# Three PSUM banks in turn, in place of two, for the gate and up products of three feed-forward layers

## The chip, the core and the metric

The kernel runs on one core of a Trainium2 chip. The metric is the device time of one execution in microseconds (us), the median of several. The core's engines run side by side and wait for one another by semaphores: TensorE (PE in the profile, its weight loads are PEld), VectorE (DVE), ScalarE (ACT), GpSimd (POOL), and SyncE (SP), which here only issues DMAs. Matmul results go to PSUM, a memory of eight banks of 512 fp32 columns in each of 128 partitions.

## The reference, cut to what matters

Two small networks follow one another over x of 256 tokens by 1024 features. The first has a mixer, a cross attention to a memory and a feed-forward layer. The second has two layers, each of an attention, a cross attention to a memory and a feed-forward layer with a short convolution. The three feed-forward layers are these (2816 hidden features, 22 blocks of 128):

```python
def _swiglu(hn, w_gate, w_up, w_down):                       # first network, here "ffn0"
    return (jax.nn.silu(hn @ w_gate) * (hn @ w_up)) @ w_down

def conv_ffn(h, w_up, conv_w, conv_b, w_down):               # second network, "ffn1", "ffn2"
    S = h.shape[1]
    u = h @ w_up
    up = jnp.pad(u, ((0, 0), (CONV_WIDTH_2 - 1, 0), (0, 0)))
    c = conv_b
    for i in range(CONV_WIDTH_2):
        c = c + up[:, i:i + S] * conv_w[i]
    gate, val = c[..., :D_FF_2], c[..., D_FF_2:]
    return (jax.nn.silu(gate) * val) @ w_down
```

## The kernel before

Activations lie feature-major, so a linear layer's output is made in blocks `m` of 128 features by 256 tokens, each of them one accumulator. Every fp32 product is made of three matmuls of rounded parts: weights and inputs are split into a high part and a rest (`w_hi`, `w_lo`; `a_hi`, `a_lo`; `b_hi`, `b_lo`), and `three` (L446) issues high by high, high by rest and rest by high. All weights pass in one fixed order through slots of eight 128 by 128 blocks: SP loads a slot to `w_raw`, ACT makes its high part (L1153), DVE (L1708) or POOL (L2522) its rest, and PE spends 24 matmuls on it. The split slots are a ring of three. Every engine's program is written out by hand in this order, and each engine works strictly in its own order; the helper `ahead(s)` on ACT and DVE makes the parts of slots up to three ahead before the work that belongs to slot `s`.

Each accumulator has a key, such as `("x_o", 7)` or `("ffn0", 3)`, and a bank (`ACC_BANK`). `accumulators` hands out banks in the order of the slots: a key in `fixed` gets that bank, every other takes the next of a cycle over banks 0 and 1. `ACC_BEFORE` is the key that had the same bank last. PE, before the first matmul of a key, waits until the engine that reads that earlier accumulator has done so:

```python
def acc_take(key):
    if ACC_BEFORE[key]:
        pe.wait_ge(*at(("acc", ACC_BEFORE[key])))
    return acc(key)
```

Where a residual is added (`x_o`, the output projection of the first cross attention, has keys 0 to 7), DVE adds accumulator `m` to `h` (L2135), which frees the bank; before it, in DVE's order, stands the rest of a later weight slot (`ahead`, L1708), and after it come `a_lo` of block `m-1` (L1720) and the running sum of squares (L2125). Block `m` of the next layer's input is ready with `a_lo` of `m`. `ffn0` follows `x_o` directly on PE. In a feed-forward layer PE's order for `f` from 0 to 22 is: gate product `f` (key 2f), up product `f` (key 2f+1), down product of `f-1`; the down products add up in banks 4 to 7. Each of these is one slot:

```python
for g in range(2):
    out = acc_take((name, 2 * f + g))[:, 0:T]
    slot_ready(s)
    for k in range(KD):
        if f == 0 and g == 0:
            pe.wait_ge(*at(("a_lo", tag, k)))
        ins = three(out, blocks(s, k), pair(A, k), k == 0, k == KD - 1)
```

After key 0, PE makes the last sum of squares in bank 2 (L533), of which ACT makes the scale `rstd` (L1184, L1186) between two loads of activation tables (L1158, L1161). DVE reads each gate and up accumulator at L2267, times `rstd`, and that read frees its bank. In `ffn1` and `ffn2` the convolution follows on ACT (L1591) and DVE (L2272, L2274); then come SiLU on ACT (L1596), the product on DVE (L2286), and its high part (L1606) and rest (L2295), which the down product reads.

Of the kernel before, what the change touches and what calls it, by code (L numbers as in the profile page):

```python
# [80 lines left out]
KIND = {name: kind for name, kind, _, _ in LINEARS}  # L81
# [2484 lines left out]

def accumulators():

    turn = itertools.cycle((0, 1))
    fixed = {("ab_v", 0, 0): 0, ("ab_v", 0, 1): 1, ("ab_q", 0): 6, ("ab_k", 0): 7, ("ab_q", 1): 6, ("ab_k", 1): 7,  # L2570
             ("ab_o", 0): 7, ("glu", 1): 3, ("glu", 2): 2, ("fox_v", 0, 0): 0, ("fox_v", 0, 1): 1, ("fox_f", 0): 6, ("fox_q", 0): 7,
             ("fox_k", 0): 6, ("fox_q", 1): 7, ("fox_k", 1): 6, ("fox_o", 0): 7}
    seen = set()
    for name, j in SLOT:
        k, m = SHAPE[name]
        if KIND[name] == "tok":
            per = k * min(m, 4) // 8
            keys = [(name, j // per, tt) for tt in range(TT)]
        elif KIND[name] == "ffn":
            keys = [(name, i) for i in range(2 * NF)]  # L2580
        else:
            keys = [(name, i) for i in range(8 * j // k, -(-8 * (j + 1) // k))]
        for key in keys:
            if key not in seen:
                seen.add(key)
                yield key, fixed[key] if key in fixed else next(turn)


ACC_BANK = dict(accumulators())
ACC_BEFORE, _last = {}, {}  # L2590
for _key, _b in ACC_BANK.items():
# [143 lines left out]
```

## Time and profile before

| | |
|---|---|
| median of 3 runs | 1244.7 us (1241.61 to 1245.04) |
| profiled execution, its own time | 1243.67 us |
| its span, first to last instruction | 1241.4 us |
| PE busy | 1188.7 us, 96% |
| PE's weight loads busy | 1117.8 us, 90% |
| DVE, ACT, POOL busy | 809.1, 656.9, 264.8 us |
| PE in the chain that ended last | 82% of the span |
| mean granted TensorE clock | 0.988 of 2.4 GHz |

A busy share is an average over the whole program: what the change is worth is read where the feed-forward layers and their neighbours stand in the trace. The three layers' gate, up and down products lie at about 316 to 507, 678 to 870 and 1035 to 1227 us of the span.

### The profile page before, as it was taken

Reading aid. Unit: us, or ns where it says so; the run is one execution under the profiler, and the core shown is the slowest. Engines: PE = TensorE matmul, PEld = TensorE weight load, DVE = VectorE, ACT = ScalarE, POOL = GpSimd, SP = SyncE. Lnnn points to the kernel's source line nnn. Section 1 sums busy time; section 2 is a strip of 40 time slices with the busy share of each in tenths; the row PEclk is TensorE's granted clock in tenths of the full one; section 3 lists DMA queues with packets and bytes.
Section 4 is the critical chain, followed back from the end, with each engine's and each line's share of the span. In section 5 each row is a group of like instructions: output and inputs, shape, how many; then the busy total and the mean of one; then the engine's idle time right before and its main releaser. Section 6 shows DMA issues by size and latency. Waiting matters only on the chain.

```text
span 1241.4 us, 24075 instructions
## 1 busy us (share of the span) xinstructions
PE 1188.7 (96%) x9808; PEld 1117.8 (90%) x9808; DVE 809.1 (65%) x1427; ACT 656.9 (53%) x1128; POOL 264.8 (21%) x171
## 2 busy tenths in 40 slices
PE   7999998999999999999989999999999988999997
PEld 5888788899999999898887999999889877999997
DVE  4897855754644554667775777776664566776776
ACT  3346455554644444555555555555655566555554
POOL 4030000211223223221130223223212111223231
PEclk9999999899999999999989999999999999999999
DMA  8333333434665555533343465655443332655551
GB/s 331 121 120 104 118 122 136 125 131 135 192 189 182 189 178 179 157 126 108 119 136 102 153 187 174 192 179 187 143 136 117 126 125 87 197 176 186 187 174 48
DMA packets 51660, 188.59 MB, mean 152 GB/s; under 512 B 5728, under 2 KB 5856, under 8 KB 51040
## 3 DMA queue, kind: packets, MB, share of 16 engines
q1 hardware_dynamic: 51552, 187.07, 47.1%
q8 instruction: 78, 1.28, 0.4%
q14 instruction: 30, 0.25, 0.1%
HBM read 186.00 MB, written 1.05 MB: 151 GB/s over the span
## 4 chain that ended last, share of the span: by engine, by line
PE 82%; DVE 8%; ACT 4%; issue 3%; POOL 2%; DMA 0%; DVEq 0%; ACTq 0%; POOLq 0%
PE banks L446 64%; PE banks L476 6%; ACT w_hi L1153 2%; DVE w_lo L1708 2%; PE banks L519 1%; PE banks L948 1%; PE banks L504 1%; POOL w_lo L2522 1%; DVE a_lo L1720 1%; DVE h L2135 1%; DVE gates L2125 1%; PE banks L962 1%; PE banks L567 1%; PE banks L928 1%; PE banks L865 1%
## 5 line engine op out<-in xcount | busy, mean ns | idle before, releaser
L446 PE MATMUL banks<-a_hi,w_hi 128*128 128x256 f32 x1432 | 412.0, 288 | 8.7 <-DVE a_lo L1720 6.3
L2522 POOL TENSOR_TENSOR w_lo<-w_raw,w_hi 128x1024 fp32r<-128x1024 f32 x98 | 238.9, 2439 | 837.7 <-ACT w_hi L1153 837.7
L1153 ACT ACTIVATE w_hi<-w_raw 128x1024 fp32r<-128x1024 f32 x313 | 328.6, 1050 | 155.1 <-PE banks L446 155.0
L446 PE MATMUL banks<-a_lo,w_hi 128*128 128x256 f32 x1432 | 406.0, 284 | 0.0
L446 PE MATMUL banks<-a_hi,w_lo 128*128 128x256 f32 x1432 | 405.8, 283 | 0.0
L1708 DVE TENSOR_TENSOR w_lo<-w_raw,w_hi 128x1024 fp32r<-128x1024 f32 x215 | 267.6, 1245 | 78.6 <-ACT w_hi L1153 78.2
L446 PEld LDWEIGHTS banks<-a_hi,w_hi 128*128 128x128 f32 x1432 | 275.5, 192 | 12.1 <-DVE a_lo L1720 7.2
L446 PEld LDWEIGHTS banks<-a_lo,w_hi 128*128 128x128 f32 x1432 | 275.6, 192 | 0.5
L446 PE MATMUL banks<-b_hi,w_hi 128*128 128x256 f32 x880 | 255.9, 291 | 21.1 <-DVE b_lo L1725 6.6
L446 PEld LDWEIGHTS banks<-a_hi,w_lo 128*128 128x128 f32 x1432 | 275.5, 192 | 0.0
L446 PE MATMUL banks<-b_lo,w_hi 128*128 128x256 f32 x880 | 250.8, 285 | 0.0
L446 PE MATMUL banks<-b_hi,w_lo 128*128 128x256 f32 x880 | 250.7, 285 | 0.0
L446 PEld LDWEIGHTS banks<-b_hi,w_hi 128*128 128x128 f32 x880 | 170.6, 194 | 26.7 <-issue 9.5
L446 PEld LDWEIGHTS banks<-b_lo,w_hi 128*128 128x128 f32 x880 | 170.7, 194 | 0.3
L446 PEld LDWEIGHTS banks<-b_hi,w_lo 128*128 128x128 f32 x880 | 170.6, 194 | 0.0
L1591 ACT ACTIVATE arena<-arena,pars 128x256 f32<-128x256 f32 x88 | 53.0, 602 | 132.1 <-DVE arena L2267 132.1
L2267 DVE TENSOR_TENSOR arena<-banks,rstd 128x256 f32<-128x256 f32 x132 | 55.9, 424 | 102.4 <-PE banks L446 92.5
L2272 DVE SCALAR_TENSOR_TENSOR arena<-arena,pars 128x255 f32<-128x255 f32 x88 | 59.7, 678 | 60.7 <-ACT arena L1591 60.7
L476 PE MATMUL banks<-early,w_raw 128*128 128x256 f32 x368 | 83.8, 386 | 7.7 <-DMA w_raw<-in_weights 7.5
L476 PEld LDWEIGHTS banks<-early,w_raw 128*128 128x128 f32 x368 | 70.2, 193 | 18.4 <-DMA w_raw<-in_weights 7.5
L1179 ACT ACTIVATE a_hi<-h,pars 128x256 fp32r<-128x256 f32 x64 | 32.5, 507 | 64.0 <-DVE h L2135 53.9
L1606 ACT ACTIVATE b_hi<-arena 128x256 fp32r<-128x256 f32 x66 | 27.6, 418 | 37.3 <-DVE arena L2286 37.3
(388 smaller groups left out, 1330.2 us busy)
## 6 DMA issues: line engine op xcount, KB each, us to landing
w_raw<-in_weights SPq DMA_DIRECT2D x342, 512.0 KB, 3.6
arena<-in_mem SPq DMA_DIRECT2D x2, 1024.0 KB, 8.9
h<-in_x SPq DMA_DIRECT2D x1, 1024.0 KB, 5.0
early<-in_mem SPq DMA_DIRECT2D x1, 1024.0 KB, 14.2
out_h<-h SPq DMA_DIRECT2D x4, 256.0 KB, 2.6
cons<-in_cons SPq DMA_DIRECT2D x1, 546.0 KB, 7.5
arena<-in_late SPq DMA_DIRECT2D x1, 448.0 KB, 4.2
pars<-in_pars SPq DMA_DIRECT2D x1, 290.5 KB, 2.9
```

The source lines that it names most:

```text
L446: ins = mm(out, l, r, start=start and n == 0, stop=stop and n == 2, skip_group_check=check)
L476: ins = mm(out, raw(s, b % 8), x[:, k, :], start=n == 0, stop=n == K - 1)
L504: ins = mm(out, x[:, k, cols], raw(s, b * w % 8, w), start=k == 0, stop=k == K - 1)
L519: ins = mm(bank[2][:, 0:T] if out is None else out, ONES_D[:] if by is None else by, squares, start=m == 0, stop=m == KD - 1)
L1153: do(WHI[:, ring(n), :], RAW[:, n % RAW_SLOTS, :], ACT.Copy).then_inc(*inc("w_hi_made", ("w_hi", n)))
L1179: do(x[0][:, m, :], src, ACT.Copy, scale=par(g, m)).then_inc(*inc("input_hi", ("a_hi", tag, m)))
L1591: do(FC[:, 2 * (f % 2) + g, :], FS[:, 2 * (f % 3) + g, :], ACT.Identity, scale=par(f"cw{conv}", 88 + g * NF + f), bias=par(f"cb{conv}", g ...
L1606: do(BH[:, f % 3, :], FA[:, f % 2, :], ACT.Copy).then_inc(*inc("ffn_act_hi", ("act_hi", tag, f)))
L1708: v.tensor_tensor(WLO[:, ring(n), :], RAW[:, n % RAW_SLOTS, :], WHI[:, ring(n), :].bitcast(F32), ALU.subtract).then_inc(*inc("w_lo_made", ...
L2267: v.tensor_tensor(x, acc(t)[:, 0:T], R[:], ALU.mult).then_inc(*inc("ffn_scaled", ("fs", tag, f, g), ("acc", t)))
L2272: step(v.scalar_tensor_tensor(c[:, 1:T], x[:, 0:T - 1], par(f"cw{conv}", 44 + g * NF + f), c[:, 1:T], ALU.mult, ALU.add), label="ffn_conv")
L2522: g.tensor_tensor(WLO[:, ring(n), :], RAW[:, n % RAW_SLOTS, :], WHI[:, ring(n), :].bitcast(F32), ALU.subtract).then_inc(*inc("w_lo_pool", ...
```

## The change

The keys of layers of the kind `"ffn"` take their bank from a cycle of their own, over banks 0, 1 and 3. All other keys go on with the cycle over 0 and 1. An instruction's place in its engine's order is the same on every engine; the bank that some matmuls and reads address differs, and so does the read for which PE waits.

```diff
 def accumulators():
 
-    turn = itertools.cycle((0, 1))
+    turn, of_three = itertools.cycle((0, 1)), itertools.cycle((0, 1, 3))
...
         for key in keys:
             if key not in seen:
                 seen.add(key)
-                yield key, fixed[key] if key in fixed else next(turn)
+                yield key, fixed[key] if key in fixed else next(of_three if KIND[name] == "ffn" else turn)
```

What the tables `ACC_BANK` and `ACC_BEFORE` hold for the first keys of the three layers and for what follows a layer, worked out from the code:

```
key            before: bank, freed by     now: bank, freed by
ffn0, 0        1   x_o, 6                 0   x_o, 7
ffn0, 1        0   x_o, 7                 1   x_o, 6
ffn0, 2        1   ffn0, 0                3   glu, 1
ffn0, 3        0   ffn0, 1                0   ffn0, 0
ffn0, 4        1   ffn0, 2                1   ffn0, 1
ffn0, 5        0   ffn0, 3                3   ffn0, 2
ffn1, 0        0   m_o0, 6                3   ffn0, 41
ffn1, 1        1   m_o0, 7                0   m_o0, 6
ffn1, 2        0   ffn1, 0                1   m_o0, 7
ffn2, 0        1   m_o1, 6                1   m_o1, 6
ffn2, 1        0   m_o1, 7                3   ffn1, 42
ffn2, 2        1   ffn2, 0                0   m_o1, 7
ab_v, 0, 0     0   ffn0, 43               0   ffn0, 42
ab_v, 0, 1     1   ffn0, 42               1   ffn0, 43
```

From key 3 on, a key of these layers waits for the read of the key three before it, where it waited for the one two before it.

## Rows read from the trace of the kernel before

**Rows 1.** The page: span, and busy time of each engine

```profile
span 1241.4 us, 24075 instructions
...
PE 1188.7 (96%) x9808; PEld 1117.8 (90%) x9808; DVE 809.1 (65%) x1427; ACT 656.9 (53%) x1128; POOL 264.8 (21%) x171
```

**Rows 2.** Stretches inside the layers: busy us by engine, granted clock, DMA share, GB/s

```profile
320.00:505.00 185.00, 184.79 (x1533) 184.19 (x1534) 92.29 (x139) 87.64 (x117) 53.01 (x23) 1.00 0.60 186
695.00:870.00 175.00, 175.00 (x1454) 175.00 (x1454) 126.74 (x203) 97.52 (x143) 50.22 (x21) 1.00 0.58 183
1055.00:1226.00 171.00, 171.00 (x1427) 171.00 (x1426) 123.75 (x199) 94.69 (x139) 48.07 (x20) 1.00 0.55 170
```

**Rows 3.** Who waited for L2267 (DVE's read of an accumulator): us, times

```profile
PEld banks L446: 0.2, 1
```

**Rows 4.** Timeline of PE, start of `ffn0`: start us, us, instruction, [idle before, releaser]

```profile
316.31 0.28 PE L446 MATMUL banks<-a_hi,w_hi 128*128 128x256 f32 x1
...
319.94 0.38 PE L446 MATMUL banks<-a_hi,w_hi 128*128 128x256 f32 x1 [1.32 <-DVE a_lo L1720]
320.17 0.28 PE L446 MATMUL banks<-a_lo,w_hi 128*128 128x256 f32 x1
...
321.02 0.27 PE L446 MATMUL banks<-a_hi,w_lo 128*128 128x256 f32 x1
321.13 0.59 PE L533 MATMUL banks<-gates,ones_d 128*128 128x256 f32 x2
```

**Rows 5.** Timeline of DVE, the same stretch and the first products

```profile
317.81 1.23 DVE L1708 TENSOR_TENSOR w_lo<-w_raw,w_hi 128x1024 fp32r<-128x1024 f32 x1 [0.98 <-ACT w_hi L1153]
318.96 0.41 DVE L2135 TENSOR_TENSOR h<-h,banks 128x256 f32<-128x256 f32 x1
319.41 0.48 DVE L1720 SCALAR_TENSOR_TENSOR a_lo<-h,pars,a_hi 128x256 fp32r<-128x256 f32 x1
...
326.96 0.42 DVE L2267 TENSOR_TENSOR arena<-banks,rstd 128x256 f32<-128x256 f32 x1
...
329.33 1.22 DVE L1708 TENSOR_TENSOR w_lo<-w_raw,w_hi 128x1024 fp32r<-128x1024 f32 x1 [0.52 <-ACT w_hi L1153]
```

**Rows 6.** Timeline of ACT, the scale `rstd` of `ffn0`

```profile
321.19 1.28 ACT L1158 ACT_TABLE_LOAD   x1
322.48 0.48 ACT L1184 ACTIVATE rstd<-banks,cons 128x256 f32<-128x256 f32 x1
```

**Rows 7.** Timeline of PE, keys 3 and the first down product of `ffn0`

```profile
327.19 0.28 PE L446 MATMUL banks<-a_hi,w_lo 128*128 128x256 f32 x1
327.43 0.39 PE L446 MATMUL banks<-a_hi,w_hi 128*128 128x256 f32 x1
...
330.28 0.28 PE L446 MATMUL banks<-a_hi,w_lo 128*128 128x256 f32 x1
330.66 0.36 PE L446 MATMUL banks<-b_hi,w_hi 128*128 128x256 f32 x1
```

**Rows 8.** Timeline of PE, elsewhere: matmuls after idle stretches of 1.7 us and more

```profile
646.72 0.58 PE L446 MATMUL banks<-a_hi,w_hi 128*128 128x256 f32 x1 [3.53 <-DVE a_lo L1720]
...
692.88 0.36 PE L446 MATMUL banks<-b_hi,w_hi 128*128 128x256 f32 x1 [1.75 <-DVE w_lo L1708]
...
1016.07 0.66 PE L1067 MATMUL banks<-cons,arena 128*128 128x128 f32 x4 [1.91 <-DVE arena L2167]
...
1049.60 0.36 PE L446 MATMUL banks<-b_hi,w_hi 128*128 128x256 f32 x1 [1.77 <-DVE w_lo L1708]
```

**Rows 9.** Stretches after such idle times: columns as in rows 2

```profile
645.40:652.30 6.90, 5.58 (x24) 5.40 (x25) 3.25 (x4) 1.84 (x3) 0.98 (x1) 0.51 0.18 71
...
693.20:696.60 3.40, 3.40 (x18) 3.40 (x17) 2.11 (x4) 2.94 (x5) 1.82 (x1) 0.50 0.53 154
1017.50:1020.90 3.40, 3.40 (x12) 2.21 (x12) 1.55 (x3) 2.00 (x6) 0.00 (x0) 0.51 0.00 0
...
1048.20:1051.60 3.40, 2.00 (x17) 2.03 (x18) 2.62 (x5) 1.59 (x3) 0.10 (x1) 1.00 0.27 73
```

## The prediction

> **What bounds the kernel now.** I read the page first. PE is busy for 96% of the span, its weight loads for 90% [rows 1]. The reader is to see that an engine other than PE can matter only where it makes PE wait. The next view is the table of stretches inside the three feed-forward layers: PE is busy for 184.79 of 185 us, 175.00 of 175 and 171.00 of 171, at a granted clock of 1.00, which is the 2.4 GHz level [rows 2]. 1454 matmuls in 175 us are one in 0.12 us, so a slot of 24 takes 2.88 us. The third view is that of the line L2267, the read that frees a gate or up accumulator: all that PE waited for it in the whole program is 0.2 us, once [rows 3]. So two banks are hardly ever too few, and the steady part of the layers has nothing to give. What is left is where a layer begins, and there I went through the timelines of PE, DVE and ACT.
>
> **The change, part by part.** From its key 3 on, every key of a layer waits for a read that DVE has done earlier in its order than the read it waited for before. Such a wait is weaker, and can only take away waiting. The bank's number itself changes no instruction's size. Two places remain: the one wait that is taken away, and the first keys of each layer.
>
> The wait that is taken away: in `ffn0`, DVE reads key 1 at 326.96 for 0.42 us, to 327.38 [rows 5], and PE starts key 3 at 327.43 [rows 7]. The matmul before started at 327.19, and at 0.12 us apart the next would have come at 327.31. So this wait is 0.12 us of PE; the most it can be is the 0.2 us of [rows 3]. It would be given back by itself in any case: the first down product starts at 330.66, 0.38 us after the matmul before it, so PE stood 0.26 us there [rows 7]. It waited for the rest of its weights, which DVE made from 329.33 for 1.22 us, to 330.55 [rows 5]. DVE made that in its own order after ACT's high part, and a PE that comes 0.12 us earlier would wait 0.38 us in place of 0.26. Taken alone, this part is worth nothing.
>
> The first keys: for `ffn1` and `ffn2` the reads waited for by keys 0 to 2 are those of earlier accumulators, or of the same as before and asked for later, by the table in the section on the change. They cost nothing. `ab_v` and the products after `ffn1` begin only when the next layer's inputs are made, long after the last gate and up reads; nothing either.
>
> Key 0 of `ffn0` is the exception. The new cycle begins at bank 0, while the old one stood at bank 1 at this point. So key 0 now waits for the read of `x_o` 7, the last residual block, where it waited for that of `x_o` 6. In the trace of before PE starts key 0 at 316.31, as soon as it is through with `x_o` 7 [rows 4], does the matmuls of the first six input blocks, and stands for 1.32 us until block 6 of the input has its rest, from 319.94 on [rows 4]. DVE reads `x_o` 7 only at 318.96 for 0.41 us, to 319.37, because the rest of a weight slot (317.81, 1.23 us) stands ahead of it in DVE's order [rows 5]. Nothing in this order needs PE's key 0: those weights were waiting for ACT. So in the changed kernel PE stands still from about 316.5 to 319.42 (a release by DVE reached PE in 0.05 us at 319.94, after the row that ended at 319.89), 2.9 us in one piece.
>
> After that it finds both late blocks ready: 24 matmuls with the first gap as in [rows 4] (319.94 to 320.17, 0.23 us) and 22 of 0.12 us put the last at 319.42 + 0.23 + 2.64 = 322.29, where it was at 321.02 [rows 4]. Key 0 starts 3.11 us later and ends **1.27 us later**; the difference is the time that PE stood inside key 0 before, and doesn't now.
>
> What of these 1.27 us stays: behind key 0 in PE's queue stand the last sum of squares, key 1, key 2, key 3 and the first down product. The two short waits at 327.43 and 330.66 give back 0.12 and 0.26 us, if what they waited for doesn't slip as much. Two things slip with the sum of squares. ACT starts `rstd` at 322.48, right when its table is loaded (321.19 + 1.28 = 322.47) [rows 6]. The sum's matmuls end at 321.13 + 0.59 = 321.72 [rows 4], so it lay ready; it now comes at 322.99 and sets the start itself, 0.51 us later, 0.55 with a release of 0.04. `rstd`, and behind it the reads, the high parts and the rests, come later by that. The down product's rest is there at 330.55 + 0.55 = 331.10. PE alone reaches it at 330.66 + 1.27 - 0.12 - 0.26 = 331.55, which is later, so PE's own time decides. The slip that stays is 331.55 - 330.66 = **0.9 us**. Its bounds are 0.55 (the slip of ACT's chain alone) and 1.27 (nothing given back). Behind that point PE runs without a gap to the end of the layer [rows 2], so no later slack takes it up, and all that follows moves with it.
>
> The granted clock: the trace has idle stretches of PE beside which the 2.9 us can be held. After 1.75 us (matmul at 692.88) the clock fell to the 1.2 GHz level for 693.20 to 696.60; it was also at it from 645.40 to 652.30, in the course of an idle time of 3.53 us and after it, and from 1017.50 on, after 1.91 us. After 1.77 us (at 1049.60) it stayed at 1.00 [rows 8, 9]. So falls begin to show at about this length, and the wait of 1.32 us at 319.94 had none: the whole stretch from 320 has a clock of 1.00 [rows 2]. At 2.9 us a fall is the likelier outcome. Its price: in 3.40 us at the lower level 18 matmuls started [rows 9] where 0.12 us each would give 28, which is 10.3 times 0.12, or 1.2 us; half of all work in 3.4 us is 1.7. I take **1.4 us**, between them. Without a fall it is 0.
>
> Sum: 0.9 + 1.4 = 2.3 us. Against the profiled execution's own 1243.67 us that is 1246.0. That execution lies 1.0 below the median of the three runs, 1244.7, and against the median it is **1247.0 us**. 0.3% is 3.7 us, and this is about what a measurement of this kernel can tell from no change; its three runs lie 3.4 us apart. So I forecast a loss too small to be told from nothing.
>
> **The rivals.**
>
> The late start without a fall of the clock: 0.9 us alone, 1245.6. For it: 1.77 us at 1049.60 without one [rows 8, 9]. Against: 2.9 us is much longer.
>
> The late start is not there, or is hidden, and the change does nothing: 1244.7. This is so if the read of `x_o` 7 comes earlier than in the trace. Against it stands DVE's order, in which the rest of a weight slot, 1.23 us, and a wait for ACT of 0.98 us before it stand ahead of the read [rows 5].
>
> The third bank does what it seems made for, and PE runs ahead where it waited for DVE: at most the 0.2 us of [rows 3], 1244.5. To be faster by over 0.3% it would need eighteen times that.
>
> Slower by over 0.3%: the clock does not come back after some 3.4 us, but stays low as at 645.40, for 6.90 us [rows 9]. By the same rate that is 2.8 us, by half of all work 3.4 us; with 0.9 it comes to 3.7 to 4.3, or 1248.4 to 1249.0. It decides from the point where the lower level lasts longer than 6.8 us. Against it: in that stretch PE did 24 matmuls in 6.90 us, while behind key 0 of `ffn0` stand hundreds without a gap, as behind 692.88, where the clock was back at 696.6.
>
> A second way to be slower is a short pause of PE at each change of bank, often enough for the clock to fall within the layers. One such fall costs 1.4 us and three pass 0.3%, 1248.9. Against it: the down products already go from bank to bank, four of them in one slot, in stretches with PE busy 175.00 of 175 us at clock 1.00 [rows 2]. This is what the Trainium skill describes on its page "TensorE: Matmul & The Clock Gate", section "A second HAM failure mode: psum-queue depth-cycling": in a kernel that cycled through PSUM banks PE paused briefly between groups of matmuls and the clock went up and down. By that rule the change would be slower here; the trace of before doesn't bear it out for cycles over two or four banks.
>
> **How the numbers follow.** Late start with one fall: 0.52. Late start without: 0.26. No change at all: 0.08. Low for longer: 0.08. Falls within the layers: 0.02. Gain from the bank: 0.04. The predicted time is that of the first. Its own range is 1247.0 with the bounds 0.55 + 1.2 and 1.27 + 1.7, that is 1246.5 to 1247.7, before the scatter of the runs. The 8 in 10 must hold the case without a fall, 1245.6, and the scatter of a median of runs, some 1.5 us to either side (the three runs reach 3.1 below and 0.3 above theirs); it leaves out most of the low ones and reaches toward the longer fall: 1243.5 to 1249.5. Slower by over 0.3%, above 1248.4, gets the two rivals' 0.10 and scatter of the likeliest, 0.13. Faster by over 0.3%, below 1241.0, is only scatter, 0.02. The rest is 0.85.
>
> **What would show it.** In the changed kernel's timeline PE's key 0 of `ffn0` starts near 319.4 with some 2.9 us idle before it, released by DVE's L2135, in place of 316.3 and 1.32 us at block 6. Its sum of squares is 1.3 us later, `rstd` 0.5 us later, the first down product 0.9 us later than 330.66, or up to 1.7 more where the stretch behind 319.4 has a clock of 0.5. L2267 appears among those waited for by PE with nothing. The starts of `ffn1` and `ffn2`, taken from each layer's first slot, look as before. I am wrong if key 0 starts before 319, if the layers' inner stretches show a clock under 1.00 beyond one fall, or if PE waits anywhere for a read that it didn't wait for before, other than that of `x_o` 7.

## The result and the profile after

Twenty executions of each kernel: 1243.93 us before (1241.22 to 1247.46), 1246.11 us after (1245.20 to 1248.04). The ratio is 1.0017, with a 95% interval from 1.0010 to 1.0024: 2.2 us slower. That is less than the 0.3% that the prediction took as the least that can be told from no change; with twenty executions it can be told, since the whole interval lies above 1. The executions also lie closer together than before: the fastest of the two kernels are 4.0 us apart, the slowest 0.6 us. The profiled execution took 1245.46 us, its span is 1243.2 us (1241.4 before).

The page of the changed kernel, in the lines that answer to [rows 1]: the busy times stay as they are to within 1 us each.

```profile
span 1243.2 us, 24075 instructions
...
PE 1189.2 (96%) x9808; PEld 1118.4 (90%) x9808; DVE 809.3 (65%) x1427; ACT 656.9 (53%) x1128; POOL 264.2 (21%) x171
```

PE's timeline at the start of `ffn0`, where [rows 4] stood. The last matmul of `x_o` 7 starts at 316.81; the first of key 0 comes 3.23 us later, after an idle time of 2.96 us that DVE's L2135 ends. The input blocks that were waited for before are not waited for any more. The matmuls then come 0.21 us apart, not 0.12.

```profile
316.81 0.28 PE L446 MATMUL banks<-b_hi,w_lo 128*128 128x256 f32 x1
320.04 0.58 PE L446 MATMUL banks<-a_hi,w_hi 128*128 128x256 f32 x1 [2.96 <-DVE h L2135]
320.42 0.41 PE L446 MATMUL banks<-a_lo,w_hi 128*128 128x256 f32 x1
320.63 0.41 PE L446 MATMUL banks<-a_hi,w_lo 128*128 128x256 f32 x1
...
324.27 0.59 PE L533 MATMUL banks<-gates,ones_d 128*128 128x256 f32 x2
```

DVE's timeline of the same place, as in [rows 5]: the read of `x_o` 7 stands behind the rest of a weight slot, and ends at 319.98.

```profile
318.43 1.23 DVE L1708 TENSOR_TENSOR w_lo<-w_raw,w_hi 128x1024 fp32r<-128x1024 f32 x1 [0.97 <-ACT w_hi L1153]
319.57 0.41 DVE L2135 TENSOR_TENSOR h<-h,banks 128x256 f32<-128x256 f32 x1
```

ACT's timeline, as in [rows 6]: the scale now waits for PE's sum of squares, 1.82 us after the table is loaded.

```profile
321.80 1.28 ACT L1158 ACT_TABLE_LOAD   x1
324.90 0.47 ACT L1184 ACTIVATE rstd<-banks,cons 128x256 f32<-128x256 f32 x1 [1.82 <-PE banks L533]
```

The first down product, as in [rows 7], follows key 3 without a gap: what it waited for before is ready.

```profile
333.21 0.28 PE L446 MATMUL banks<-a_hi,w_lo 128*128 128x256 f32 x1
333.33 0.28 PE L446 MATMUL banks<-b_hi,w_hi 128*128 128x256 f32 x1
```

The table of stretches (us; busy us and instructions of PE, PEld, DVE, ACT, POOL; granted clock, DMA share, GB/s). The clock stands at the 1.2 GHz level for 3.4 us, from 319.60 on, near the end of the idle time; the inside of the three layers is as full as in [rows 2], at 1.00.

```profile
319.60:323.00 3.40, 2.96 (x14) 2.96 (x15) 1.94 (x6) 2.96 (x4) 1.14 (x1) 0.51 0.65 225
...
323.20:505.00 181.80, 181.80 (x1516) 181.75 (x1515) 90.26 (x134) 83.98 (x112) 49.55 (x22) 1.00 0.60 182
697.00:872.00 175.00, 175.00 (x1453) 174.80 (x1451) 126.95 (x203) 97.34 (x143) 49.91 (x21) 1.00 0.60 182
1057.00:1228.00 171.00, 171.00 (x1427) 171.00 (x1426) 123.73 (x199) 94.71 (x139) 48.10 (x20) 1.00 0.55 170
```

Who waited for L2267, the read of a gate or up accumulator, as in [rows 3]: PE is gone from the list, and only ACT is left.

```profile
ACT arena L1591: 132.1, 86
ACT arena L1596: 0.7, 1
```

Executions drift against one another before this place: the last matmul of `x_o` 7 starts at 316.19 before, at 316.81 after, and between 312.94 and 318.07 in the traces below. So from here on I measure one distance inside each trace, **D**: from the start of the last matmul of `x_o` 7 to that of the first down product of `ffn0`. Before it is 330.66 - 316.19 = 14.47 us, after 333.33 - 316.81 = 16.52 us. The 2.05 us between them are the change. Behind that point the rest of the program to its last instruction takes 0.9 us less in the trace of after. That difference lies at one place. Before, the clock is at the lower level from 645.40 to 652.30 [rows 9], 6.90 us; after, at the same place, for 3.4 us:

```profile
649.35 0.39 PE L446 MATMUL banks<-a_hi,w_hi 128*128 128x256 f32 x1 [3.53 <-DVE a_lo L1720]
...
650.60:654.00 3.40, 3.40 (x19) 3.40 (x18) 1.65 (x2) 1.68 (x3) 0.00 (x0) 0.50 0.03 7
...
694.54 0.36 PE L446 MATMUL banks<-b_hi,w_hi 128*128 128x256 f32 x1 [1.75 <-DVE w_lo L1708]
```

From the first of these matmuls to the last it is 45.19 us after and 692.88 - 646.72 = 46.16 us before. Both executions idle for 3.53 us ahead of it, and each wait of PE of 0.3 us and more between the two is as long as before to 0.01 us. So how long the clock stays low at one and the same place differs from execution to execution, and the total time of a single execution says little about a change of 2 us.

### The profile page after: what moved, and what is told of

It is laid out like the page before. It is cut to its first block, busy times and chain, and to the rows that moved or that the text cites. A ratio compares the mean times of both kernels' runs of the same rounds, so it can differ in the third digit from the quotient of the medians.

```text
span 1243.2 us, 24075 instructions
## 1 busy us (share of the span) xinstructions
PE 1189.2 (96%) x9808; PEld 1118.4 (90%) x9808; DVE 809.3 (65%) x1427; ACT 656.9 (53%) x1128; POOL 264.2 (21%) x171
## 4 chain that ended last, share of the span: by engine, by line
PE 84%; DVE 7%; ACT 4%; issue 3%; POOL 1%; DMA 0%; SPq 0%; DVEq 0%; ACTq 0%
PE banks L446 64%; PE banks L476 7%; ACT w_hi L1153 2%; DVE w_lo L1708 2%; PE banks L519 2%; PE banks L948 1%; PE banks L504 1%; POOL w_lo L2522 1%; DVE h L2135 1%; DVE a_lo L1720 1%; PE banks L962 1%; PE banks L567 1%; PE banks L928 1%; PE banks L865 1%; PE banks L842 1%
## 5 line engine op out<-in xcount | busy, mean ns | idle before, releaser
L1708 DVE TENSOR_TENSOR w_lo<-w_raw,w_hi 128x1024 fp32r<-128x1024 f32 x215 | 267.6, 1245 | 78.7 <-ACT w_hi L1153 78.3
L2267 DVE TENSOR_TENSOR arena<-banks,rstd 128x256 f32<-128x256 f32 x132 | 55.9, 424 | 104.4 <-PE banks L446 92.7
L1720 DVE SCALAR_TENSOR_TENSOR a_lo<-h,pars,a_hi 128x256 fp32r<-128x256 f32 x64 | 45.1, 705 | 4.2 <-ACT a_hi L1179 2.3
```

The source lines that it names most:

```text
L1708: v.tensor_tensor(WLO[:, ring(n), :], RAW[:, n % RAW_SLOTS, :], WHI[:, ring(n), :].bitcast(F32), ALU.subtract).then_inc(*inc("w_lo_made", ...
L1720: v.scalar_tensor_tensor(x[1][:, m, :], src, par(g, m), x[0][:, m, :].bitcast(F32), ALU.mult, ALU.subtract).then_inc(*inc("input_lo", ("a_ ...
L2267: v.tensor_tensor(x, acc(t)[:, 0:T], R[:], ALU.mult).then_inc(*inc("ffn_scaled", ("fs", tag, f, g), ("acc", t)))
```

## The experiments

The theory: the loss is the wait of `ffn0`'s key 0 for the read of `x_o` 7, about 0.9 us of late start and about 1.4 us of a fall of the granted clock that follows the idle time; the third bank itself is worth nothing either way. The main rival: cycling over three banks costs something of its own.

**Where the cycle begins.** The first three kernels change only the banks of the cycle (the comments are mine).

```diff
-    turn, of_three = itertools.cycle((0, 1)), itertools.cycle((0, 1, 3))
+    turn, of_three = itertools.cycle((0, 1)), itertools.cycle((1, 0, 3))   # first kernel
+    turn, of_three = itertools.cycle((0, 1)), itertools.cycle((0, 1))      # second
+    turn, of_three = itertools.cycle((0, 1)), itertools.cycle((3, 0, 1))   # third
```

> Three banks in turn, but the cycle begins at bank 1 (1, 0, 3), so that key 0 of ffn0 again waits for the read of x_o 6 and all later keys still have three banks. My theory (the whole loss is key 0 of ffn0 waiting for the read of x_o 7): level with the kernel before, 1243.9 us, ratio 1.0000 within 0.0007, key 0 starting near 316.3 right behind x_o 7. Rival (the third bank itself costs, by pauses at each change of bank): 1.0017 as in the changed kernel.

> Two banks as before, but the layers have a cycle of their own that begins at bank 0 in ffn0: no third bank, only the wait of key 0 for the read of x_o 7. My theory: the full loss, ratio 1.0017 (1246.1 us), PE idle for about 2.96 us ahead of key 0. Rival (the loss comes with the third bank): 1.0000.

> Three banks, the cycle begins at bank 3 (3, 0, 1): key 0 of ffn0 waits for nothing recent, key 1 for the read of x_o 7, which is over (319.4 in the trace of before) long before key 1 comes up at 321.4. My theory: level with before, 1.0000. Rival (any key behind x_o 7 in its bank is late): 1.0017.

Measured: 1.0006 (0.9996 to 1.0016) for 1, 0, 3; 1.0017 (1.0007 to 1.0027) for two banks from 0; 1.0002 (0.9991 to 1.0014) for 3, 0, 1. The second is the one that settles it: no third bank, the same loss, and the same idle time in PE's timeline:

```profile
314.90 0.28 PE L446 MATMUL banks<-b_hi,w_lo 128*128 128x256 f32 x1
318.15 0.58 PE L446 MATMUL banks<-a_hi,w_hi 128*128 128x256 f32 x1 [2.96 <-DVE h L2135]
...
331.52 0.28 PE L446 MATMUL banks<-b_hi,w_hi 128*128 128x256 f32 x1
```

Its D is 331.52 - 314.90 = 16.62 us. The third kernel has a D of 331.54 - 316.75 = 14.79, 0.32 us more than before. The banks don't explain that: in its trace DVE begins the read of `x_o` 7 later against PE. From the start of the last matmul of `x_o` 7 to that read it is 3.09 us here and 3.10 us in the first kernel's trace, but 2.76 to 2.78 us in those of before, after, and two banks from 0:

```profile
319.84 0.41 DVE L2135 TENSOR_TENSOR h<-h,banks 128x256 f32<-128x256 f32 x1
...
320.83 0.39 PE L446 MATMUL banks<-a_hi,w_hi 128*128 128x256 f32 x1 [1.65 <-DVE a_lo L1720]
```

So D too has a scatter of some 0.3 us, and kernels are best compared where this delay is the same. The first is less clean than I expected. Key 0 starts right behind `x_o` 7, at 317.51 behind 317.33, and yet D is 333.20 - 317.33 = 15.87. That is 1.40 us more than before, and 1.08 us more than the third kernel, which has the same delay of DVE's read. PE's idle time inside key 0 was 1.49 us, and in this profiled execution it was followed by a fall of the clock. The table of stretches for it:

```profile
322.60:326.00 3.40, 3.40 (x16) 3.22 (x15) 0.42 (x1) 3.32 (x5) 2.36 (x1) 0.51 0.71 274
```

So a fall at this place needs no 2.96 us. That the kernel before has some here too, though its one profiled execution had none, is likely, but not shown. The intervals of the first and the third kernel end at 1.0016 and 1.0014, just short of the 1.0017 of the rival, and can't tell a cost of 0.1% from none; that key 0 isn't late is read from the traces.

**The two parts of the loss, apart.** In the changed kernel PE gets work that nothing needs, just where it would stand idle:

```diff
             for g in range(2):
+                if name == "ffn0" and f == 0 and g == 0:
+                    for _ in range(23):
+                        mm(bank[3][:, 0:T], AH[:, 0, 0:P], AH[:, 0, :], start=True, stop=True)
                 out = acc_take((name, 2 * f + g))[:, 0:T]
```

> The changed kernel with 23 extra matmuls of 128x256 into bank 3 (their result is overwritten unread) ahead of key 0 of ffn0, 2.8 us of work inside the 2.96 us for which PE stands there. They take no time from anything that is needed, but PE isn't idle. My theory (0.9 us late start, the rest of the loss a fall of the granted clock after the idle stretch): ratio 1.0007 (1244.8 us), no stretch at clock 0.5 near 320. Rival (the clock has no part, all 2.2 us are the late start and what follows it): 1.0017.

Measured: 1.0010 (1.0000 to 1.0020), 1245.34 us. In PE's timeline the extra matmuls fill the gap, and key 0 still waits for the same read:

```profile
318.07 0.28 PE L446 MATMUL banks<-b_hi,w_lo 128*128 128x256 f32 x1
318.19 2.92 PE L891 MATMUL banks<-a_hi 128*128 128x256 f32 x23
321.31 0.39 PE L446 MATMUL banks<-a_hi,w_hi 128*128 128x256 f32 x1 [0.20 <-DVE h L2138]
...
333.35 0.28 PE L446 MATMUL banks<-b_hi,w_hi 128*128 128x256 f32 x1
```

The clock is 1.00 throughout (320 to 335 us):

```profile
320.00:335.00 15.00, 14.80 (x122) 14.54 (x121) 8.54 (x15) 10.27 (x14) 4.63 (x2) 1.00 0.50 168
```

D is 333.35 - 318.07 = 15.28: 0.81 us more than before. The delay of DVE's read is the same 2.77 us as in the traces of before and after, so this is the late start alone, and the other 16.52 - 15.28 = 1.24 us of the changed kernel are the fall of the clock. In the measured medians the interval holds both the expected 1.0007 and, at its edge, the rival's 1.0017; the two traces tell them apart, the medians don't.

**The read itself.** If key 0 waits because DVE makes the rest of a weight slot first, then a read ahead of it must shorten the wait. The edit, on the changed kernel and on the kernel before, for `x_o` 7 alone:

```diff
                 for m in range(KD):
-                    ahead(FIRST[name] + (m * K + K - 1) // 8)
+                    if name != "x_o" or m < KD - 1:
+                        ahead(FIRST[name] + (m * K + K - 1) // 8)
                     t = (name, m)
                     dve.wait_ge(*at((name, m)))
                     step(v.tensor_tensor(H[:, m, :], H[:, m, :], acc(t)[:, 0:T], ALU.add),
                          ("h", tag, m), ("acc", t), label="h_made")
                     if m:
                         lo_gained(tag, m - 1, A, H[:, m - 1, :], g)
                         square_sum(tag, m - 1)
+                    ahead(FIRST[name] + (m * K + K - 1) // 8)
```

> The changed kernel, but DVE reads x_o 7 (and makes input block 6) ahead of the rest of the weight slot, not behind it. My theory (the wait of key 0 is as long as DVE is late with this one read, 319.4 in place of about 316.9): key 0 starts near 316.9, only 0.6 us late, input block 6 is ready when PE comes to it, the 1.3 us idle of before vanishes too; ratio to before between 0.9988 and 1.0002, most likely 0.9992. Rival (the read is late for another reason, PE's own product or ACT): 1.0017.

> The kernel before with the same edit of DVE's order at x_o 7 alone. My theory: the idle 1.32 us ahead of input block 6 goes, some 1.0 us of it stays won: ratio 0.9992 (1243.0 us). Rival (the start of the layer is bound by ACT's table load and the rests behind it, so that PE's gain is given back at the first down product): 0.9998 to 1.0000.

Measured: 0.9984 (0.9973 to 0.9995) and 0.9977 (0.9964 to 0.9989). Both beat the kernel before, and by more than I expected. In the first one's PE timeline the idle time ahead of key 0 is 1.09 us in place of 2.96 us:

```profile
317.79 0.28 PE L446 MATMUL banks<-b_hi,w_lo 128*128 128x256 f32 x1
319.16 0.39 PE L446 MATMUL banks<-a_hi,w_hi 128*128 128x256 f32 x1 [1.09 <-DVE h L2136]
...
331.19 0.28 PE L446 MATMUL banks<-b_hi,w_hi 128*128 128x256 f32 x1
```

D is 13.40 us here, and 329.90 - 316.62 = 13.28 us on the kernel before: 1.07 and 1.19 less than 14.47. Neither trace has a fall near 320. With this order the bank of key 0 matters by 0.12 us, since what it waits for then lies in front of an old wait that is there anyway. Of the 0.16% and 0.23%, 1.1 us is 0.09%; the rest would be falls of the clock that the kernel before has at this place in some of its executions. I infer that from the run of banks 1, 0, 3; no run counts them, and it isn't shown.

**The same order everywhere.** The kernel before, with the condition `if m == 0` in place of the one above, so in all six residual projections; then that kernel with the weight slot's rest at block 7 also behind the last input block.

> The kernel before with that order in every residual block of all six residual projections from block 1 on: first the read, then the rest of the next weight slot. PE waited 3.9 us in four places for these reads in the trace of before. My theory: up to 5 us less, ratio 0.9965. Rival (the rests of the weights then come late and PE waits for them in place of the reads): 1.0000 or slower, up to 1.003.

Measured: 0.9939 (0.9920 to 0.9958), 1236.72 us, more than the 0.9965 expected. The views of who waited for whom (us in all, times, longest) show where PE waits less. Before:

```profile
PE banks L446 <- DVE a_lo L1720: 6.8, 5, 3.5
...
PE banks L446 <- POOL w_lo L2522: 4.5, 5, 1.3
PE banks L446 <- DVE h L2135: 3.9, 4, 1.2
```

In this kernel (the read is now L2136):

```profile
PE banks L446 <- DVE a_lo L1720: 5.6, 5, 2.4
...
PE banks L446 <- DVE h L2136: 1.5, 2, 0.8
```

The waits for the reads fell by 2.4 us. More, 4.5 us, comes from the waits for POOL's weight rests, which are gone from the list and which I hadn't expected to change; why they went, no run separates. At `x_o` itself it was no gain. In DVE's timeline block 7's `a_lo` took 2.59 us, where the block before it took 0.48:

```profile
317.83 1.22 DVE L1708 TENSOR_TENSOR w_lo<-w_raw,w_hi 128x1024 fp32r<-128x1024 f32 x1
318.96 2.59 DVE L1720 SCALAR_TENSOR_TENSOR a_lo<-h,pars,a_hi 128x256 fp32r<-128x256 f32 x1
```

It ran beside this instruction in POOL's timeline, and ended when that had ended:

```profile
318.94 2.34 POOL L2524 TENSOR_TENSOR w_lo<-w_raw,w_hi 128x1024 fp32r<-128x1024 f32 x1 [11.99 <-ACT w_hi L1153]
```

PE stood 2.45 us for it and the clock fell after that, so that D was 332.62 - 316.32 = 16.30. The next kernel moves the weight rest:

```diff
                         square_sum(tag, m - 1)
-                    ahead(FIRST[name] + (m * K + K - 1) // 8)
+                    if m < KD - 1:
+                        ahead(FIRST[name] + (m * K + K - 1) // 8)
                 lo_gained(tag, KD - 1, A, H[:, KD - 1, :], g)
                 square_sum(tag, KD - 1)
+                ahead(FIRST[name] + (K * KD - 1) // 8)
```

> The kernel before with every residual read ahead of the next weight rest (as in the run before this one), and at block 7 also the last input block's rest (L1720) ahead of it. In that run L1720 of block 7 in ffn0 took 2.59 us in place of 0.48 while POOL worked from 318.94 to 321.28, and PE stood 2.45 us for it. My theory: ahead of POOL's instruction it takes 0.48 us, PE's wait inside key 0 is under 0.7 us, and the kernel gains another 1 to 2 us at this place: ratio to the kernel before 0.9925. Rival (the weight rest then falls beside POOL's instruction, takes as long, and PE waits for that at key 1): 0.9939 as in that run.

Measured: 0.9911 (0.9893 to 0.9929), 1232.70 us, the fastest kernel with two banks; the rival's 0.9939 is outside the interval. The same `a_lo` takes 0.48 us again, and PE has no idle time there; D is 327.80 - 315.49 = 12.31.

```profile
317.00 0.48 DVE L1720 SCALAR_TENSOR_TENSOR a_lo<-h,pars,a_hi 128x256 fp32r<-128x256 f32 x1
317.40 0.42 DVE L2125 TENSOR_TENSOR gates<-gates,squares 128x256 f32<-128x256 f32 x1
317.73 1.22 DVE L1708 TENSOR_TENSOR w_lo<-w_raw,w_hi 128x1024 fp32r<-128x1024 f32 x1
```

**Three banks on the new order.** Two kernels were meant to try this on the fastest one.

> The same DVE order, with banks 1, 0, 3 in turn for the feed-forward layers. My theory (a third bank has nothing to win even where the start of a layer is tighter): level with the two-bank kernel of this order, within 0.0008. Rival (with the residual out of the way, PE's waits for gate and up reads show, and three banks take them away): 0.0010 or more faster than the two-bank one.

> The same DVE order, with banks 0, 1, 3 in turn as in the changed kernel, so that key 0 of ffn0 waits for the read of x_o 7. The read now comes about 0.8 us after PE ends x_o 7. My theory: PE idles some 0.7 us there, of which 0.3 to 0.7 us stay: ratio 0.0003 to 0.0006 above the kernel with banks 1, 0, 3, far less than the 0.0017 of the change on the old order. Rival (the loss is the same with any order of DVE): 0.0017 above it.

They were built on the kernel with 0.9939, not on the one with 0.9911, so the texts above name the wrong base, and what they are to be held beside is 0.9939. Measured: 0.9937 (0.9920 to 0.9954) for banks 1, 0, 3 and 0.9936 (0.9917 to 0.9954) for 0, 1, 3. So no gain or loss from three banks can be seen there, and none from the bank of key 0; the intervals are too wide for the 0.03% to 0.06% expected. In the traces, the 0.51 us of idle time ahead of key 0 is made up in front of the slow `a_lo`, for which PE stood 1.74 us in place of 2.44. The two on the right base:

> The DVE order of the fastest kernel so far (all residual reads first, and at block 7 the last input block's rest ahead of the weight rest; ratio 0.9911 with two banks), now really with banks 1, 0, 3 in turn: the two runs before had the weight rest ahead of that input block. My theory: level with two banks on this order, 0.9911 within 0.0010, key 0 behind x_o 7 without a gap, the first down product some 12.3 us behind the last matmul of x_o 7. Rival (three banks win or lose something of their own where the start is tight): off by more than 0.0015.

> The same order with banks 0, 1, 3 as in the changed kernel. PE waits for the read of x_o 7, 0.5 us idle as in the run with the other DVE order, but here neither an old wait inside key 0 nor much slack behind it can take that back. My theory: some 0.6 us later than banks 1, 0, 3, ratio 0.9916. Rival (the cost of the bank is the 0.0017 of the changed kernel whatever the order): 0.9928.

Measured: 0.9905 (0.9888 to 0.9922), 1233.68 us, and 0.9913 (0.9896 to 0.9929), 1234.97 us, beside 0.9911 of two banks. In the traces, D is 325.24 - 312.94 = 12.30 for banks 1, 0, 3, the same as with two, and 328.44 - 315.61 = 12.83 for 0, 1, 3, that is 0.53 us more. The latter's key 0 in PE's timeline:

```profile
315.61 0.28 PE L446 MATMUL banks<-b_hi,w_lo 128*128 128x256 f32 x1
316.40 0.39 PE L446 MATMUL banks<-a_hi,w_hi 128*128 128x256 f32 x1 [0.51 <-DVE h L2136]
```

The medians of the three kernels lie within each other's intervals, and the last one's interval holds the rival's 0.9928 too. The rival is settled by D, one trace for each kernel: it gives the third bank 0.0 us, and its wrong start 0.5 us. DVE's read begins 0.31 to 0.32 us behind the last matmul of `x_o` 7 in all three traces, so they can be compared. The distances of all kernels:

```
kernel                                   D, us    idle ahead of key 0 (inside it)    clock fell near 320
before (banks 0, 1)                      14.47    none (1.32)                        no
changed (0, 1, 3)                        16.52    2.96                               yes
banks 1, 0, 3                            15.87    none (1.49)                        yes
two banks, from 0                        16.62    2.96                               yes
banks 3, 0, 1                            14.79    none (1.65)                        no
changed, PE kept busy                    15.28    filled but for 0.20                no
changed, x_o 7 read first                13.40    1.09                               no
before, x_o 7 read first                 13.28    none (0.80)                        no
before, all reads first                  16.30    none (2.45)                        yes
the same with 1, 0, 3                    16.15    none (2.44)                        yes
the same with 0, 1, 3                    14.83    0.51 (1.74)                        no
all reads first, weight rest last        12.31    none                               no
the same with 1, 0, 3                    12.30    none                               no
the same with 0, 1, 3                    12.83    0.51                               no
```

## Why the prediction held, point by point

**The steady part has nothing to give.** Right. PE is busy for 175.00 of 175 us in both traces, and in the tightest order D is the same to 0.01 us in the one trace with two banks and the one with three.

**The wait of 0.12 us at key 3 is worth nothing.** As forecast the one wait for a gate read is gone, and the first down product was the next thing to be waited for: the run with banks 3, 0, 1 shows it waiting again, at 331.54 behind 330.96. Its size could not be seen in a time.

**Key 0 waits for the read of `x_o` 7.** Right in place and in size: 2.96 us idle, forecast 2.9. The run with two banks from 0 shows that it is this wait and not the third bank.

**0.9 us of it stays.** 0.81 was measured, with PE kept busy. In that trace key 0's last matmul starts at 324.17, 6.10 us behind the last of `x_o` 7. Before it was 321.02 - 316.19 = 4.83 us, so key 0 ends 1.27 us later, as forecast. The waits behind it gave back 0.46 us, where 0.38 was forecast. The first down product followed without a gap, and PE's own time set it, not ACT's chain.

**The clock falls, at 1.4 us.** It fell, for 3.4 us, and cost 1.24 us in the changed kernel and 1.08 us in the run with banks 1, 0, 3, held beside banks 3, 0, 1. So the term was 0.2 to 0.3 us too large. What the prediction had wrong is that it read a length at which falls begin from single waits, and so took the kernel before to be free of falls at this place. That "the wait of 1.32 us at 319.94 had none" was true of one execution; an idle time of 1.49 us in another had one. The two waits of [rows 8] that the forecast leaned on, 1.75 us with a fall and 1.77 us without, come out the other way round in the trace of banks 3, 0, 1:

```profile
693.13 0.36 PE L446 MATMUL banks<-b_hi,w_hi 128*128 128x256 f32 x1 [1.75 <-DVE w_lo L1708]
1049.98 0.36 PE L446 MATMUL banks<-b_hi,w_hi 128*128 128x256 f32 x1 [1.76 <-DVE w_lo L1708]
...
693.00:697.00 4.00, 3.11 (x24) 2.94 (x24) 2.62 (x6) 3.14 (x5) 1.97 (x1) 1.00 0.43 131
...
1051.40:1054.80 3.40, 3.31 (x17) 3.04 (x16) 2.69 (x4) 2.25 (x4) 2.38 (x1) 0.50 0.35 130
```

So the same wait is followed by a fall in one execution and not in another, and the right cost of the fall is some 1.2 us times how much oftener it comes. How often the kernel before has one there stays open: one profile for each kernel doesn't tell. That its executions scatter with the clock is seen in eleven of them in one job: the fastest took 1240.5 us at a mean granted clock of 0.994, the slowest 1246.0 at 0.987.

**The sum.** That the loss agrees to 0.1 us (2.2 measured in the medians, 2.3 forecast) is in part luck, since the forecast counted one whole fall and none before. The time itself was forecast 0.9 us too high, 1247.0 for 1246.11, and lies below the 1246.5 to 1247.7 that the prediction called its own range before scatter. 0.8 us of that is the start: the median of three runs was 1244.7, that of twenty 1243.93.

**The rivals.** No change at all, and a gain from the bank, are both out by the interval. So is the late start without any fall, 0.9 us or a ratio of 1.0007 where the interval begins at 1.0010. A longer low clock didn't come. Short pauses at each change of bank didn't either: PE was busy for 171.00 of 171 us at a clock of 1.00 in the last layer. What the Trainium skill describes on its page "TensorE: Matmul & The Clock Gate", section "A second HAM failure mode: psum-queue depth-cycling", isn't borne out for three banks here.

## What to carry to other kernels

When a resource is handed out by a cycle, a change of its length also changes who comes first: look at the neighbours where the cycle begins, not only at its steady state. Before adding a buffer, read who waits for the release; here it was 0.2 us in 1241, and a run with the old number of banks and the new start told the two apart in one step. Where an engine waits for an accumulator's read, ask what stands ahead of the read in the reader's own order: to move 1.2 us of work that isn't urgent behind it, in six projections, gave 0.6%, and 0.9% with the last input block also ahead, some four to five times what the change had lost. Not all of that comes from the reads: PE's waits for POOL's rests went too. Before taking a length of idle time as safe or not for the clock, look for the same wait in more than one trace.

## What was unexpected of the hardware

A DVE instruction (L1720), mostly 0.48 us long, took 2.59 us when it began 0.02 us after a POOL tensor_tensor of 2.34 us, and ended 0.27 us after that. At this place it happened in three traces (2.59, 2.59 and 2.61 us). It didn't need the new order: the trace of before has six such instructions of 2.25 to 2.56 us, each begun while POOL worked and ended 0.27 to 0.29 us after POOL. One of them is what PE's longest idle time in [rows 8], 3.53 us ahead of 646.72, waited for (the first line is two instructions of POOL, the second of which was at work):

```profile
641.22 5.17 POOL L2522 TENSOR_TENSOR w_lo<-w_raw,w_hi 128x1024 fp32r<-128x1024 f32 x2 [6.68 <-ACT w_hi L1153]
644.11 2.56 DVE L1720 SCALAR_TENSOR_TENSOR a_lo<-h,pars,a_hi 128x256 fp32r<-128x256 f32 x1
```

With all reads first there are thirteen. The other way round, where DVE's L1708 began at 317.73 and POOL's instruction at 318.10, DVE kept its 1.22 us and POOL's took 3.10 us in place of 2.34. So in these traces the second to begin waits for the whole of the first. The Trainium skill has this as a rule, on its page "SBUF — State Buffer", section "Who interferes with whom": a DVE instruction with two inputs from SBUF and a GpSimd instruction that reads SBUF need the same port, and the later one is blocked until the earlier is done. The traces agree, with the numbers above. What I had not expected is that an order chosen to free one wait could put a short instruction that PE waits for right behind one of POOL's.
